# Turning x by products with a diagonal of inverse deviations, and one difference of x moved ahead of the discretisation

## What is computed

```python
def rms_norm(x, g):
    y = xf * lax.rsqrt(jnp.mean(xf * xf, axis=-1, keepdims=True) + EPS)
    return (y * g.astype(F32)).astype(x.dtype)
...
xn = rms_norm(h, mix_norm_g[l])
proj = jnp.einsum('bsd,de->bse', xn, w_in[l])
q_a, k_a, v_a, u_s5, q_h, f_h, i_h, g_h = jnp.split(proj, split_at, axis=-1)
```

## Time and profile before

| | |
|---|---|
| median of 3 executions | 1982.48 us (1981.11 to 1984.16) |
| the profiled execution, its own time | 1982.84 us |
| its span, first to last instruction | 1980.0 us |
| mean granted TensorE clock | 0.954 |
| TensorE busy | 1791.9 us, 91% of the span |
| VectorE busy | 788.3 us, 40% |
| ScalarE busy | 248.2 us, 13% |
| chain that ended last | PE 71%, DMA 20%, DVE 4% |

### The profile page before, as it was taken

The page is one execution under the profiler, slowest core; times in us unless marked ns, Lnnn a source line. Parts: engine busy times, 40 slices in busy tenths (PEclk is TensorE's granted clock), DMA queues, the critical chain, the costliest instruction groups (busy, mean ns, idle before and its releaser), DMA issues.

```text
span 1980.0 us, 30734 instructions
## 1 busy us (share of the span) xinstructions
PE 1791.9 (91%) x12867; PEld 1139.0 (58%) x12867; DVE 788.3 (40%) x1516; ACT 248.2 (13%) x580; POOL 178.8 (9%) x204
## 2 busy tenths in 40 slices
PE   6999999999999989999355899999999999999666
PEld 4888999789997879999311233333333333333222
DVE  7666595277467544333400122221222222223015
ACT  3012111200325331000200000000000000000004
POOL 1453342000000000000100000000000000000000
PEclk9999999999999999999677899999999999999888
DMA  5343333321222232221699999999999999999996
GB/s 216 109 130 92 90 104 87 98 65 43 65 70 75 70 146 86 65 85 44 289 423 421 425 425 422 423 423 422 418 422 412 420 423 426 417 423 423 408 405 225
DMA packets 80393, 506.58 MB, mean 256 GB/s; under 512 B 18785, under 2 KB 23029, under 8 KB 46977
## 3 DMA queue, kind: packets, MB, share of 16 engines
q1 hardware_dynamic: 62706, 480.40, 60.4%
q0 software_dynamic: 5152, 15.81, 2.4%
q10 hardware_dynamic: 12400, 8.36, 1.7%
HBM read 498.32 MB, written 12.99 MB: 258 GB/s over the span
## 4 chain that ended last, share of the span: by engine, by line
PE 71%; DMA 20%; DVE 4%; issue 2%; ACT 1%; SPq 1%; ACTq 0%; DVEq 0%; POOL 0%; POOLq 0%
PE psum L958 20%; PE psum L1269 17%; PE psum L961 15%; DMA arena<-in_moe_w_gate 14%; PE psum L1233 6%; PE psum L1296 3%; DMA arena<-in_moe_w_up 3%; DMA arena<-in_moe_w_down 3%; PE psum L1116 2%; DVE arena L1704 2%; PE psum L1017 1%; PE psum L1363 1%; PE psum L1375 1%; DVE arena L1707 1%; DMA arena<-hs_rows,arena 1%
## 5 line engine op out<-in xcount | busy, mean ns | idle before, releaser
L1269 PE MATMUL psum<-arena 128*32 128x512 f32 x3584 | 423.1, 627 | 82.4 <-DMA arena<-in_moe_w_gate 34.6
L958 PE MATMUL psum<-arena 128*128 128x128 f32 x3584 | 412.6, 277 | 3.5 <-issue 3.5
L958 PEld LDWEIGHTS psum<-arena 128*128 128x128 f32 x3584 | 407.0, 193 | 10.9 <-issue 10.4
L1704 DVE TENSOR_TENSOR arena<-psum,arena 128x512 f32<-128x512 f32 (+1 forms) x319 | 211.7, 680 | 402.1 <-PE psum L1233 379.5
L1269 PEld LDWEIGHTS psum<-arena 128*32 128x32 f32 x3584 | 120.4, 115 | 378.0 <-issue 376.9
L961 PE MATMUL psum<-arena 128*128 128x256 f32 x1456 | 322.4, 380 | 1.1 <-DVE arena L1704 1.1
L961 PEld LDWEIGHTS psum<-arena 128*128 128x128 f32 x1456 | 273.4, 190 | 39.0 <-issue 2.1
L1704 DVE TENSOR_TENSOR arena<-arena,psum 128x256 f32<-128x256 f32 (+2 forms) x172 | 75.1, 437 | 473.0 <-PE psum L958 217.1
L1296 PE MATMUL psum<-arena 128*32 128x512 f32 x1664 | 185.9, 605 | 20.9 <-DMA arena<-in_moe_w_down 20.6
L1704 DVE TENSOR_TENSOR arena<-arena 128x240 f32<-128x240 f32 (+17 forms) x464 | 187.4, 446 | 33.0 <-ACT arena L1424 25.2
L1233 PE MATMUL psum<-arena 128*128 128x512 f32 x416 | 192.4, 605 | 0.0
(11 more groups left out here) (213 smaller groups left out, 993.0 us busy)
## 6 DMA issues: line engine op xcount, KB each, us to landing
arena<-in_moe_w_gate SPq DMA_DIRECT2D x64, 2048.0 KB, 28.0
arena<-in_moe_w_up SPq DMA_DIRECT2D x64, 2048.0 KB, 26.3
arena<-in_moe_w_down SPq DMA_DIRECT2D x60, 2048.0 KB, 27.9
arena<-in_w_in SPq DMA_DIRECT2D x86, 512.0 KB, 4.6
arena<-in_w_out SPq DMA_DIRECT2D x32, 512.0 KB, 4.6
arena<-in_x SPq DMA_DIRECT2D x8, 1024.0 KB, 8.3
hs_rows<-arena ACTq DMA_DIRECT2D x4, 1024.0 KB, 4.8
arena<-in_moe_w_down SPq DMA_DIRECT2D x4, 1024.0 KB, 15.2
```

The lines of the kernel that those rows point to most:

```text
L958: last = mm(B(bank, [(1, P)], off=t * P), F(a + t * P, P), F(w + i * P, P), start=start and t == 0, stop=(i == KH - 1), skip_group_check=True)
L1269: last = mm(B(bank, [(1, FE)], 32 * g, 32), F(XT + c * CAP + 32 * g, 32), F(SLOT[slot] + (c % 8) * FE, FE), start=(c == 0), stop=(c == KD ...
L1704: return v.tensor_tensor(o, a, b, op)
```

## The change

Three edits.

1. For row blocks 0, 1 and 2, VectorE no longer scales the block. It writes the identity times the block's inverse deviations, a 128x128 diagonal matrix (`DG`, in space that the S5 layer uses later), and signals `diag_ready`. TensorE multiplies the unscaled block by that diagonal, with a plain matmul in place of a transpose, so that the product is both turned and scaled.
2. Row block 3 is scaled by ScalarE in place (a Copy with one scale for each partition) after VectorE has taken all four reciprocals, and turned by transposes as before. The places on VectorE at which the four inverses are made are (0, 0), (0, 1), (1, 1) and (1, 3). ScalarE's wait for the gains is gone; TensorE's wait for the identity is gone and VectorE has one in its place.
3. S3 is computed right after weight sum 1 of pair 0, ahead of the discretisation, and no longer after weight sum 3.

```diff
+        DG = CA
...
                 if kind == "xT":
                     t, q = s[1:]
-                    once(ident_in, 16)
-                    once(x_scaled, t + 1)
+                    if t < TB - 1:
+                        once(diag_ready, t + 1)
+                    else:
+                        once(x_scaled, 1)
                     for c in range(4):
-                        last = tr(B(bank, [(1, P)], off=c * P), V(XRAW + t * D + 4 * q + c, [(KD, P)]), ident)
+                        x = V(XRAW + t * D + 4 * q + c, [(KD, P)])
+                        if t < TB - 1:
+                            last = mm(B(bank, [(1, P)], off=c * P), x, F(DG + t * P, P), start=True, stop=True)
+                        else:
+                            last = tr(B(bank, [(1, P)], off=c * P), x, ident)
...
                 deviation([F(XRAW + t * D, D)], F(JUNK_X, D), SSQ + t, STD + t, D).then_inc(x_std, 1)
-            act.wait_ge(gains_in, 16)
+            act.wait_ge(diag_ready, TB)
+            h = F(XRAW + (TB - 1) * D, D)
+            A(h, h, ACT.Copy, scale=F(RST + TB - 1, 1)).then_inc(x_scaled, 1)
...
+            DIAG_AT = [(0, 0), (0, 1), (1, 1), (1, 3)]
+            dve.wait_ge(ident_in, 16)
...
-                    for t1 in [0] * ((t, q) == (0, 0)) + [t + 1] * (q == 1 and t + 1 < TB):
+                    if (t, q) in DIAG_AT:
+                        t1 = DIAG_AT.index((t, q))
                         dve.wait_ge(x_std, t1 + 1)
-                        settle(v.reciprocal(F(RST + t1, 1), F(STD + t1, 1)))
-                        ts(F(XRAW + t1 * D, D), F(XRAW + t1 * D, D), F(RST + t1, 1), None, M).then_inc(x_scaled, 1)
+                        if t1 < TB - 1:
+                            settle(v.reciprocal(F(RST + t1, 1), F(STD + t1, 1)))
+                            ts(F(DG + t1 * P, P), F(IDENT, P), F(RST + t1, 1), None, M).then_inc(diag_ready, 1)
+                        else:
+                            v.reciprocal(F(RST + t1, 1), F(STD + t1, 1)).then_inc(diag_ready, 1)
...
                         weight_sum(dve, v, 0, 0)
                         weight_sum(dve, v, 0, 1)
+                        dve.wait_ge(u0_lo, 1)
+                        tt(F(S3, KH * HB), F(A11, KH * HB), F(A21, KH * HB), SU).then_inc(xsum_ready, 1)
                         disc_a()
                         disc_b()
...
-                elif s == ("pq", "u", 0, 2):
-                    dve.wait_ge(u0_lo, 1)
-                    tt(F(S3, KH * HB), F(A11, KH * HB), F(A21, KH * HB), SU).then_inc(xsum_ready, 1)
```

More of the change, by code:

```diff
@@ L480, in build @@
         x_in = [sem(f"x_in{i}") for i in range(TB)]
-        x_std, x_scaled, ident_in = sem("x_std"), sem("x_scaled"), sem("ident_in")
+        x_std, diag_ready, x_scaled, ident_in = sem("x_std"), sem("diag_ready"), sem("x_scaled"), sem("ident_in")
         disc_act, disc_dve, disc_done = sem("disc_act"), sem("disc_dve"), sem("disc_done")
```

## The result

The changed kernel takes 1989.43 us (1987.42 to 1990.64, 9 runs) against 1983.65 us (1981.11 to 1984.16, 9 runs) of the kernel before: ratio 1.0032, 95% interval 1.0024 to 1.0041. It is slower by some 6 us. The forecast was 1981.4, and its range ended at 1985.4. The profiled execution took 1989.68 us, its span 1987.9.

The account below looks back on a forecast made before the run. TensorE was taken to hold the chain, with time won before 47.95 us reaching the end. The head's 0.1 us plus 0.95 from moving S3 made 1.05, say 1.1 us, giving 1981.4 us, range 1978.2 to 1985.4.

Parts of the forecast that it names:

- What bounds the kernel: Whole kernel: TensorE holds 71% of the chain; a microsecond won before 47.95 us should reach the end.
- Two signs: Wrong if xT ends before 24 or after 27 us, or experts' first load isn't about 1 us earlier than 964.56.
- TensorE's side: Head, blocks 0 to 2: 96 matmul instructions, 19 at half pace to 13.3 us, then 77 at 0.112 taking 8.6.
- edit 1: Head: diagonal products for blocks 0 to 2 and block 3 scaled on ScalarE; gives about 0.1 us.
- the sum: Head: block 2 done at 21.9 us, five evictions remaining from 22.2, head ends at 25.25 against 25.37.
- the second case: Blocks 0 to 2: half pace lasts longer; 1983.5 us (chance 0.2), or worse (0.04), 1989.1 if held throughout.
- the rule on the clock: TensorE at the start: skill page says transposes don't count as busy for the clock; prediction said the trace disagrees.
- Edit 2: Before product 2: S3 moved ahead of the discretisation; product 2 starts at about 47.0 instead of 47.95, gaining 0.95 us.
- ScalarE's Copy: Block 3 scaling: starts at 18.5 us, takes 2.0, ends at 20.5, hidden with a cover of 1.4 us.
- The diagonal: VectorE's head: each 128x128 tensor_scalar replacing a scaling of 1.30 us takes 0.22 us, ends 0.21 and 0.25.
- the third case: Head: matmuls issued once, not twice, so VectorE bounds; 3.7 us earlier, 1977.8 with S3's move; chance 0.04.
- The fourth: Head: matmuls raise the clock earlier than transposes, full pace from 11 us, 1.2 us more: 1980.2; chance 0.04.

Follow-up runs that it names:

- Experiment 3: Changed kernel with channels laid out contiguously, weights and gains to match: 1981.0 us against 1982.13 for the kernel before, ratio 0.9996.
- experiment 4: Changed kernel with the step of the weight load's columns varied from bank to bank, output wrong: 3109.45 us, not comparable, only the head is read.
- experiment 8: Kernel before with S3 ahead of the discretisation and block 3 scaled by ScalarE, no products: 1979.7 us against 1983.25, ratio 0.9983.

## Why the prediction was wrong, point by point

**What bounds the kernel** held. What the first 48 us lose or gain goes through to the end in the main: 7.33 us at product 2, 7.9 in the span, 5.8 between the medians. Two signs that the prediction had named as showing it wrong came up: xT ended at 33.6 us (30.50 + 3.08), after 27, and the experts' first load was 8.9 us later, not 1 us earlier.

**The step that failed** is "TensorE's side" of edit 1, in its words "Real matmuls of this size late in the kernel: (18.13 - 0.27) / 159 = 0.112". Size was right and the way of reading was not: the products at 829 us read contiguous operands, those of the changed kernel a column in every 64 bytes. The term 77 x 0.112 = 8.6 us had to be 77 x 0.218 = 16.8. These 8.2 us are nearly all of the 8.3 by which chunk u 0 was later than the sum implied (33.84 against 25.5). None of the rows that were read has a plain matmul with such a step; there are only transposes with one, which hardly pay, and plain products without one. Experiment 3 took away the step and nothing else, and 7.8 us went. The bounds of that term (0.112 to 0.118) came from those two rows, and the operation was like neither: an unseen operation should have had 0.213, the slowest row of the same size, as its upper end. With it the range would have reached up to the 1989.1 of the second case.

**A rule was at hand.** The trace shows the fast, middle and slow steps of experiment 4 at 1 and 2, at 3, and from 4 elements on. The Trainium skill, "SBUF — State Buffer", in its note on cachelines, says that a line holds 16 bytes and that reads keep full speed only if at least two of them fall into one line. By that, steps of 1 and 2 float32 elements are free and 4 is not, with which the plain float32 products agree. The note itself names 4 float32 as how far one may stride for free; if that means a step of 4, this case disagrees (0.234 us). The transposes at step 16 (0.111 us) disagree, and bfloat16 agrees only in where its spacing begins to grow. The prediction weighed the rule on the clock and missed this one, which spoke against the change.

**The second case** gave 1989.1 us for products at 0.213 us all through, and 1989.43 came. That the time came out was luck; the reason was wrong. The clock did rise, at about 15.5 us, as the shorter matmuls show. Its chance of 0.04 was put on a persisting clock; the same spacing had a second cause that I had not thought of, and 0.213 and 0.218 happen to lie close together.

**Edit 2** held: 0.85 us measured alone, 0.95 forecast; the wait left is 0.2 us and is weight sum 2's, as said. **ScalarE's Copy** took 2.00 us (forecast 2.0) and was hidden. Its start, 22.56, followed the slow products. **The diagonal** took 0.29 us where 0.22 stood, outside the ends of 0.21 and 0.25. The doubling of instructions, 96 for 48 calls, was right, and so the third case is out. The fourth (matmuls raise the clock earlier) is not borne out: here it rose at about 15.5 us, before at about 14.3. But one trace of each can't settle it, since the moment moves without the change too: in experiment 8, which begins with the same 32 transposes as the kernel before, they were still (0.84 - 0.42) / 2 = 0.21 us apart at 15.33. With the contiguous layout the head came out as the sum had it but for the clock: 26.00 for chunk u 0 where 25.5 was implied, with half pace for longer than the 4.1 us taken.

**What stays open**: why a transpose with a step of 64 bytes hardly pays (0.118 us against 0.111 contiguous) and a plain float32 matmul pays in full on either side. A float32 matmul is issued twice, a transpose once, and bfloat16 once; that fits, but no run took the split apart from the mode. Nor was it settled what sets the length of the half pace at the start: 4.1 us before, 6.2 in the changed kernel (9.26 to 15.5).

## What to carry to other kernels

Before a transpose is turned into a product, look at how its operands are read: the plain float32 products measured here (128x128x128) kept their pace up to a step of 2 elements, took about 1.6 times as long at 3 and twice as long from 4 on, on either side, and the layout that hardly mattered to the transposes decides. Price an operation that the trace doesn't have by rows with the same engine, size and access pattern; if a row lacks the pattern, its slowest relative is the upper end. When two engines alternate, move work only until the other is the bound: here a single block's scaling moved to an idle third engine (ScalarE) brought chunk u 0 forward from 25.62 to 24.25 us, what 48 clever products could not do even at full pace (26.00).

## What the runs showed of the hardware that was not expected

- A plain 128x128x128 float32 matmul instruction is spaced 0.112 us with steps of 1 element, 0.119 with 2, 0.175 with 3, 0.234 with 4, 0.236 with 8 and 0.218 with 16, as stationary operand; 0.114, 0.116, 0.173, 0.227, 0.234 and 0.217 with 1, 2, 3, 4, 8 and 16 as moving one. A float32 transpose has 0.111 to 0.118 with a step of 16.
- A bfloat16 matmul goes from 0.056 to 0.063 us at a step of 16 bytes and stays there.
- The slow spacing doesn't move with TensorE's clock: 0.219 us at half pace and 0.218 at full pace with a step of 16. A spacing of 0.21 to 0.22 at a kernel's start is therefore no proof of a low clock. The duration of a matmul tells (423 against 382 ns), and so does the next group's pace.
